# A two-block layer kernel: side work of the norm, the recurrent branch, the gates and the query and key sums put at other places of the order

## The reference

```
# first block
yg = (y.reshape(b, s, SSM_INNER) * jax.nn.silu(u_z))
yg = yg.reshape(b, s, SSM_GROUPS, SSM_INNER // SSM_GROUPS)
yg = yg * lax.rsqrt(jnp.mean(yg * yg, axis=-1, keepdims=True) + RMS_EPS)
y_a = yg.reshape(b, s, SSM_INNER) * norm_w             # gated norm
y_b = h * gelu(u_ly)                                   # recurrent branch
g = sigmoid(u_g.reshape(b, s, N_BRANCHES, D_MODEL) + gate_b)
merged = g[:, :, 0, :] * (y_a @ w_proj_ssm) + g[:, :, 1, :] * (y_b @ w_proj_lru)
# second block
q, k = _l2norm(silu(q)), _l2norm(silu(k))              # query and key sums
proj = einsum("btnc,ncd->btnd", stack([y_a, y_b, y_c, y_m]), w_up)
merged = sum(sigmoid(gate_logits.reshape(B, T, N_BRANCH, D)) * proj, axis=2)
```

## Time and profile before

| | |
|---|---|
| median of three runs | 921.43 us |
| the profiled execution | 918.49 us |
| its span, first to last instruction | 916.7 us |
| mean granted TensorE clock | 0.988 |
| TensorE busy (matmuls) | 880.7 us, 96% |
| VectorE busy | 636.8 us, 69% |
| ScalarE busy | 503.9 us, 55% |
| GpSimd busy | 77.0 us, 8% |
| DMA | 148.96 MB, mean 162 GB/s |

### The profile page before, as it was taken

How to read it: one execution, slowest core, us unless ns; L and a number is a source line. 1 busy time by engine, 2 the same in 40 slices (tenths; PEclk the granted TensorE clock), 3 DMA queues, 4 the chain that set the end, 5 groups by cost and what they waited for, 6 DMA issues and landing times.

```text
span 916.7 us, 15149 instructions
## 1 busy us (share of the span) xinstructions
PE 880.7 (96%) x6082; PEld 808.8 (88%) x6082; DVE 636.8 (69%) x1122; ACT 503.9 (55%) x792; POOL 77.0 (8%) x81
## 2 busy tenths in 40 slices
PE   6979999989999999999998998999999999999997
PEld 6979999989989999999996988999999777778885
DVE  6797987977878766566568895747555545666665
ACT  5555777645367656566568764424535424354543
POOL 0200002021020211111112003000000000000000
PEclk9999999989999999999999999999999999999999
DMA  9438433547454755555553546333333332346551
GB/s 346 148 135 292 154 139 115 183 144 271 140 185 163 246 170 187 199 176 189 192 182 127 182 162 227 127 108 115 98 110 99 105 120 83 124 143 217 191 162 46
DMA packets 40446, 148.96 MB, mean 162 GB/s; under 512 B 4506, under 2 KB 4664, under 8 KB 39736
## 3 DMA queue, kind: packets, MB, share of 16 engines
q1 hardware_dynamic: 40376, 147.99, 47.8%
HBM read 146.90 MB, written 1.08 MB: 161 GB/s over the span
## 4 chain that ended last, share of the span: by engine, by line
PE 80%; DVE 12%; ACT 5%; issue 2%; DMA 1%; SPq 0%; DVEq 0%; ACTq 0%
PE bank L603 36%; PE bank L598 14%; PE bank L599 14%; PE bank L600 14%; DVE t_wl L1700 4%; DVE t_arena L1715 3%; PE bank L606 2%; DVE t_arena L1705 1%; ACT t_arena L1228 1%; ACT t_wh L1223 1%; ACT t_hh L1228 1%; DVE t_sm L1712 1%; DVE t_x L1715 1%; DMA t_x<-in_xin 1%; DVE t_arena L1986 0%
## 5 line engine op out<-in xcount | busy, mean ns | idle before, releaser
L1700 DVE TENSOR_TENSOR t_wl<-t_raw,t_wh 128x1024 fp32r<-128x1024 f32 x260 | 316.7, 1226 | 128.2 <-ACT t_wh L1223 127.6
L598 PE MATMUL bank<-t_hh,t_wh 128*128 128x256 f32 x1240 | 360.9, 291 | 7.8 <-DVE t_wl L1700 4.1
L600 PE MATMUL bank<-t_hh,t_wl 128*128 128x256 f32 x1240 | 352.4, 284 | 0.0
L599 PE MATMUL bank<-t_hl,t_wh 128*128 128x256 f32 x1240 | 352.3, 284 | 0.0
L1223 ACT ACTIVATE t_wh<-t_raw 128x1024 fp32r<-128x1024 f32 x260 | 272.6, 1058 | 130.5 <-PE bank L600 72.1
L598 PEld LDWEIGHTS bank<-t_hh,t_wh 128*128 128x128 f32 x1240 | 239.3, 193 | 12.2 <-issue 6.1
L599 PEld LDWEIGHTS bank<-t_hl,t_wh 128*128 128x128 f32 x1240 | 239.4, 193 | 0.8
L600 PEld LDWEIGHTS bank<-t_hh,t_wl 128*128 128x128 f32 x1240 | 239.1, 193 | 0.0
L603 PE MATMUL bank<-t_wh,t_br 128*128 128x512 f32 x384 | 124.1, 393 | 2.2 <-ACT t_arena L1228 2.0
L1715 DVE SCALAR_TENSOR_TENSOR t_arena<-bank,t_par,t_arena 128x255 f32<-128x255 f32 (+1 forms) x180 | 73.4, 472 | 40.5 <-ACT t_arena L1228 40.5
L603 PEld LDWEIGHTS bank<-t_wh,t_br 128*128 128x128 f32 x384 | 72.1, 188 | 19.5 <-ACT t_arena L1228 2.9
(11 more groups left out here) (138 smaller groups left out, 858.4 us busy)
## 6 DMA issues: line engine op xcount, KB each, us to landing
t_raw<-in_ws SPq DMA_DIRECT2D x260, 512.0 KB, 4.0
t_br<-decay SPq DMA_DIRECT2D x1, 2048.0 KB, 10.4
t_arena<-in_post SPq DMA_DIRECT2D x3, 512.0 KB, 4.8
t_arena<-gates SPq DMA_DIRECT2D x1, 1536.0 KB, 10.5
t_x<-in_xin SPq DMA_DIRECT2D x4, 256.0 KB, 5.9
t_bd<-in_bd SPq DMA_DIRECT2D x1, 1024.0 KB, 11.3
t_x<-in_xtok SPq DMA_DIRECT2D x1, 1024.0 KB, 6.4
t_arena<-in_mem SPq DMA_DIRECT2D x1, 1024.0 KB, 9.7
```

The costliest lines, as they stand in the source:

```text
L598: e.matmul(o, wh, xh, start=first, stop=False, skip_group_check=True)
L599: e.matmul(o, wh, xl, start=False, stop=False, skip_group_check=True)
L600: return e.matmul(o, wl, xh, start=False, stop=last, skip_group_check=True)
L1700: e.tensor_tensor(WL[q % NS][:, :], RAW[q % NR][:, :], WH[q % NS][:, :].bitcast(F), SUB).then_inc(*lo.now(q))
```

## The change

It moves side work between ticks and engines; the arithmetic and the unit stream are the same.

- Norm: the gate products stand one per tick (45 to 48), the squares one per tick (46 to 49), the group sums at 49 and 51. TensorE's column sums are at tick 53, behind pl0's first unit, the spread at 55, the multiplies at 56 and 57, and the high and low halves behind pl2. SP's three loads stand two fetches later and wait for the sums too.
- Recurrent branch: the four low halves are made by VectorE at ticks 47 to 50.
- Gates at the end: for the second chunk the tangents stand before the last tick's lanes.
- Query and key sums: all eight tiles at tick 163.

VectorE's order ahead of pl0, before: from the split difference of tick 45 to the root chain's first step (t_wl is a split difference; waits on s_ssd_dve are gate products, on s_lru_act the branch's products, on s_ssd_act group sums).

The diff:

```diff
--- before.py
+++ after.py
@@ -479,7 +479,7 @@
         g_dn = tally("dn_pool")
         p_lru, a_lru, d_lru, g_lru = tally("lru_pe"), tally("lru_act"), tally("lru_dve"), tally("lru_pool")
         a_ya, d_ya, g_ya = tally("ya_hi"), tally("ya_lo"), tally("ya_lo2")
-        a_yb, g_yb = tally("yb_hi"), tally("yb_lo")
+        a_yb, d_yb = tally("yb_hi"), tally("yb_lo")
         a_mg, d_mg = tally("merged_hi"), tally("merged_lo")
         d_mem, a_mh, g_mh = tally("mem_normed"), tally("mem_hi"), tally("mem_lo")
         a_ns, d_ns, p_ht = tally("row_square"), tally("row_added"), tally("h_turned")
@@ -549,9 +549,10 @@
             e.dma_start(MSK, masks).then_inc(s_msk, 16)
             e.dma_start(bdT[:, :, :], bd).then_inc(s_bd, 16)
             for q in range(NR, NU):
-                if q == LAST["g7"] + NS + NR:
+                if q == LAST["g7"] + NS + NR + 2:
                     e.wait_ge(*p_ssd.of("y", 7))
                     e.wait_ge(*d_ssd.of("gated", 3))
+                    e.wait_ge(*p_ssd.of("gsum"))
                     e.dma_start(XT, xtok).then_inc(s_xt, 16)
                     e.dma_start(MEMF, min_).then_inc(s_mem, 16)
                     e.dma_start(POSTW["mixpost"], post[0]).then_inc(s_post["mixpost"], 16)
@@ -772,12 +773,12 @@
                 for t in range(8):
                     yield from walk.until(T_HEAD + 2 * t + 4)
                     y_pair(t)
-                yield from walk.until(48)
+                yield from walk.until(53)
                 e.wait_ge(*d_ssd.of("gsum", 1))
                 for g in range(2):
                     m = column_sums(3, 2 * g, [SSQ[:, 4 * g + k, :] for k in range(2)], g == 0, g == 1)
                 m.then_inc(*p_ssd.now("gsum"))
-                yield from walk.until(49)
+                yield from walk.until(55)
                 e.wait_ge(*d_rs.of("ssd"))
                 e.wait_ge(*d_ssd.of("cb", 1))
                 for g in range(2):
@@ -832,8 +833,6 @@
                 ps = dn_bank("nq")
                 e.wait_ge(*a_dn.of("sq", 1))
                 for t in range(8):
-                    if t == 4:
-                        yield
                     m = column_sums(ps, 2 * t, [DSQ[:, t, :]], t == 0, t == 7)
                 m.then_inc(*p_dn.now("nq"))
                 for i in range(4):
@@ -1099,7 +1098,7 @@
             walk.tick()
 
 
-            e.wait_ge(*g_yb.of(3))
+            e.wait_ge(*d_yb.of(3))
             for i in range(4):
                 chunk(f"pl{i}", YBh, YBl)
             e.wait_ge(*d_ya.of(6))
@@ -1339,8 +1338,8 @@
                     yield from walk.until(T_HEAD + h)
                     e.wait_ge(*d_ssd.of("seg", h))
                     act(DEC[h % 8], DEC[h % 8], ACT.Exp).then_inc(*a_ssd.now("exp", h))
-                yield from walk.until(45)
                 for t in range(4):
+                    yield from walk.until(46 + t)
                     sl = slice(2 * t, 2 * t + 2)
                     e.wait_ge(*d_ssd.of("gated", t))
                     act(SSQ[:, sl, :], XBC[:, sl, :], ACT.Square).then_inc(*a_ssd.now("sq", t))
@@ -1548,12 +1547,12 @@
 
             for i in range(4):
                 walk.cols(f"pl{i}")
-                if i == 1:
+                if i == 2:
                     for k in range(8):
                         e.wait_ge(*d_ssd.of("ya", k))
                         act(Hh[:, k, :], XBC[:, k, :], ACT.Copy).then_inc(*a_ya.now(k))
             e.wait_ge(s_mem, 16)
-            e.wait_ge(*g_yb.of(3))
+            e.wait_ge(*d_yb.of(3))
             for i in range(4):
                 act(MEMQ[:, 2 * i:2 * i + 2, :], MEMF[:, 2 * i:2 * i + 2, :], ACT.Square).then_inc(*a_sq.now("mem", i))
             for i in range(4):
@@ -1667,7 +1666,11 @@
                         if hf == 0 and i == SPLIT_AT[n]:
                             split_branch(at, n)
                         name = f"gt{n}_{hf}_{i}"
-                        walk.cols(name)
+                        if i == 0:
+                            walk.cols(name)
+                    walk.unit()
+                    walk.tick()
+                    walk.unit()
                     for tt in range(2):
                         e.wait_ge(*tokens_done(name, tt))
                         if at > 0:
@@ -1943,21 +1947,21 @@
                 skip(6)
                 yield from walk.until(44)
                 skip(7)
-                yield from walk.until(45)
                 for t in range(4):
+                    yield from walk.until(45 + t)
                     sl = slice(2 * t, 2 * t + 2)
                     e.wait_ge(*d_ssd.of("y", 2 * t + 1))
                     e.wait_ge(*d_ev.of(f"z{t}"))
                     stt(XBC[:, sl, :], XBC[:, sl, :], 0.5, ZS[:, sl, :], MUL, MUL).then_inc(*d_ssd.now("gated", t))
-                yield from walk.until(47)
                 for g in range(2):
+                    yield from walk.until(49 + 2 * g)
                     e.wait_ge(*a_ssd.of("sq", 2 * g + 1))
                     tt(SSQ[:, 4 * g:4 * g + 2, :], SSQ[:, 4 * g:4 * g + 2, :], SSQ[:, 4 * g + 2:4 * g + 4, :],
                        ADD).then_inc(*d_ssd.now("gsum", g))
-                yield from walk.until(48)
+                yield from walk.until(53)
                 rsqrt("ssd", NW, 3, 4, 512, p_ssd.of("gsum"))
                 for k in range(8):
-                    yield from walk.until(50 + k // 2)
+                    yield from walk.until(56 + k // 4)
                     if k == 0:
                         e.wait_ge(*p_ssd.of("grow"))
                     g = k // 4
@@ -1991,6 +1995,11 @@
                     e.wait_ge(*d_lru.of("h", q))
                     e.wait_ge(*a_lru.of("gelu", q))
                     tt(y, y, LY[:, 2 * q:2 * q + 2, :], MUL).then_inc(*d_lru.now("y", q))
+                for q in range(4):
+                    yield from walk.until(47 + q)
+                    sl = slice(2 * q, 2 * q + 2)
+                    e.wait_ge(*a_yb.of(q))
+                    tt(YBl[:, sl, :], XC[:, sl, :], YBh[:, sl, :].bitcast(F), SUB).then_inc(*d_yb.now(q))
                 yield
 
             def rows_lane():
@@ -2401,11 +2410,6 @@
                     sl = slice(2 * q, 2 * q + 2)
                     e.wait_ge(*a_lru.of("root"))
                     tt(ti[:, sl, :], ti[:, sl, :], XC[:, sl, :], MUL).then_inc(*g_lru.now("bx", q))
-                for q in range(4):
-                    yield from walk.until(45 + q)
-                    sl = slice(2 * q, 2 * q + 2)
-                    e.wait_ge(*a_yb.of(q))
-                    tt(YBl[:, sl, :], XC[:, sl, :], YBh[:, sl, :].bitcast(F), SUB).then_inc(*g_yb.now(q))
                 yield
 
             def rows_lane():
```

## The result

The changed kernel took **908.47 us** (median of four runs, 907.85 to 910.34), the kernel before beside it 920.93 (four runs, 919.01 to 922.85): a ratio of 0.9868, 95% interval 0.9842 to 0.9894, faster by 1.3%. The forecast was 911.3 in a range of 908.5 to 917.0, so the result is the range's low end itself, once rounded, and lies under the 909 to 913 that were given for the case in which all three parts come out as worked out. The profiled executions are closer to the working: 918.49 before, 907.85 after, 10.6 us less, where 10.1 were worked out.

The account below looks back on a forecast made before the run. TensorE, busy 880.7 of 916.7 us, was taken as the bound, so only its waits and low-clock time could be won: 7.0 - 0.4 + 1.5 + 2.0 = 10.1 us off the 921.43 median gave 911.3, range 908.5 to 917.

Parts of the forecast that it names:

- all three parts come out as worked out: The main forecast, gains at norm, query and key sums and last gates: 911.3 us, range 909 to 913, chance 0.51.
- A: Gated norm's column sums moved behind pl0's first unit: 4.01 us wait, 2.31 and 0.67 lost to the clock, 7.0 gained.
- less 0.4: Charge for pl0 waiting on the recurrent branch's last low half; ends 0 and 2.7 us.
- comes out about even with 2.95: VectorE's load before pl0: 3.3 us in the fullest unit, 2.6 in its neighbours, against a 2.95 us TensorE unit.
- Rival 2: VectorE pays for the low halves: pl0 waits 2.7 us instead of 0.4, time 913.6; chance 0.14.
- The slack before ps0, 2.9: Norm's low halves Hl end at 216.7, ps0 begins at 219.6: 2.9 us slack, no charge, but thin.
- rivals 3 and 4: 3: stall only moves to pl0, 917.9, chance 0.11. 4: VectorE's lateness paid twice, before pl0 and ps0, slower, chance 0.04.
- B: Query and key sums in one burst: row spread 1.5 us earlier, 1.0 of the 2.54 us wait remains, gain 1.5.
- a sign of being wrong: A wait over 2 us at pl0's or ps0's first matmul, or clock 0.50 behind the long burst.
- rival 1: The long burst of query and key sums lowers the clock: loses 1.1 us instead of gaining 1.5, 913.9; chance 0.2.
- C: Last projection's gates: tangents before their tick's side work remove two TensorE waits of 1.00 us, gain 2.0.
- the lower end: For the last projection's gates: gain 0, if ScalarE, waiting for the unit's end, starts something else late.

Follow-up runs that it names:

- e5: Changed kernel with the norm's column sums back before the first recurrent unit, products, squares and low halves kept as changed: 915.64 us, ratio 0.9953.
- e4: Changed kernel with the four gate products and their squares in one piece at tick 45 again: 910.36 us, ratio 0.9895.
- e3: Changed kernel with the recurrent branch's four low halves back on GpSimd, at ticks 45 to 48: 910.35 us, ratio 0.9880.
- e8: Changed kernel with the query and key sums one tick earlier (162), in one group of 32 records: 908.16 us, ratio 0.9874.
- e7: Changed kernel with the query and key sums one tick earlier (162) and in two halves again: 906.58 us, ratio 0.9867.
- e2: Changed kernel with the gates' tangents behind the side work of both ticks, as before the change: 910.76 us, ratio 0.9898.
- c1: The same kernel as e7, run again: 907.33 us, ratio 0.9858.
- c0: The changed kernel run once more, unaltered: 908.26 us, ratio 0.9886.
- e9: Changed kernel keeping only the norm sums' and spread's new place; products and squares in one piece, low halves on GpSimd, group sums at tick 47: 909.78 us.
- e1: Changed kernel with the query and key sums in two halves again: 910.42 us, ratio 0.9894.

## Why the prediction was right

**Where TensorE stands, not how much it does.** The reading from the earlier trace rows held: the matmuls are the same and the waits are gone.

**A, "4.01 + 2.31 + 0.67 = 7.0 us go", less 0.4.** That is 6.6; measured 6.76, once the start's 0.55 is taken off. e5 loses 7.5 with the sums put back and the companions kept. The clock term is right too: no window between 187 and 205 is below 1.00, and e4 shows the clock's price when a wait of 2.2 comes back. The new wait was put at 0.4 and is 0.32, in the row that was named; e3, without it, is 0.6 shorter, so it costs more than its bracket says.

**VectorE's load, "comes out about even with 2.95".** The fullest unit takes 2.94 us, not the 3.3 of the working. Rival 2 (VectorE pays for the low halves) wanted a wait of 2.7 before pl0; it is 0.32. VectorE's load is even lighter for the move, since GpSimd beside it had cost 1.1 us an operation. The prediction had set this against the rival only in passing. Still the rival was right about the sign: the low halves in VectorE's order are what TensorE waits for, and with GpSimd place A is 0.6 us shorter (e3). The move was not needed.

**The slack before ps0, 2.9.** It is 2.5: VectorE's last group of Hl ends at 215.86 (212.26 + 3.60), ps0 starts at 218.40. Nothing waited there, nor for SP's loads. With that, rivals 3 and 4 have no ground: the wait did not move, and nothing was late twice.

**B, "Gain 1.5", is the step that failed, in two ways.** The time: 0.9 was gained. The sums did come earlier by half a unit, 1.42 us, but "VectorE is idle and follows at once, so the row spread comes 1.5 us earlier" took the root chain's length for fixed. It was 3.98 us before and 4.50 after, and lies between 3.30 and 4.66 in the fourteen traces; that takes 0.52. The clock: the rest of the wait was to be 1.0 with the clock at 1.00; it is 0.31 with the clock at 0.50, which the prediction itself had named as a sign of being wrong. That is rival 1's mechanism, without its price: the rival charged the slow unit with 2.3 us, of which a wait of 1.0 hides part, and here the wait for the longer chain hides all of it. That this misreading of the clock cost nothing is luck; with no wait beside it the burst costs 1.47 us (e8 against e7), the whole gain. The choice against rival 1 went by 2.54 us of idle behind two groups of 16 that had not lowered the clock. That row is about idle time, and e8 shows that no idle is needed., put aside, were the nearer ones: same kind of records, no idle, clock 0.50. The Trainium skill, "TensorE: Matmul & The Clock Gate", section "Why this matters for your kernels", names idle gaps between bursts of matmuls as what lowers the clock in mid-kernel. The runs show a fall without one (e8), and the measurement decides.

**C, "1.00 us twice".** It is 1.29 twice (e2). The wait as the trace names it starts at the end of an overlapping matmul and leaves 0.3 out; the lower end did not come.

**The total.** 6.8 + 0.9 + 2.6 = 10.2 us by places, where 10.1 were forecast. So close a sum is partly luck: 0.6 too much in B and 0.6 too little in C cancel. That the medians differ by 12.5 is in how an execution stands to its median: the profiled one before lay 2.4 us under it, the one after 0.6 under. The size of the profiled gain was right; carrying it over to the median cost 1.8 us, and with it nearly the range. Why the two kernels' profiled executions lie so differently is not shown: of the kernel before only one was traced.

## What to carry to other kernels

Where the busiest engine waits for a short reduction in the middle of a dense stream, look for a product that does not need it and put the sums behind that: the place of the sums brought 5.9 us of 6.8 here. Do not gather one-column matmuls into one group to save a wait of a microsecond; issuing them a tick earlier, in two groups, takes the wait (all of it in e7, all but 0.34 in c1) and keeps the clock. GpSimd slows VectorE (1.1 us an operation here), and a lighter VectorE still helps only if what TensorE waits for comes sooner: the low halves on VectorE came later. The kernel with the sums early and split and the low halves on GpSimd was not run; e3 and e7 make it the next to try. And price a wait by the starts of the matmuls around it, not by its bracket: 1.00 in the bracket was 1.28.

## What was not expected of the hardware

- The granted clock fell to the 1.2 GHz level with TensorE busy in every window (e8), behind 32 one-column records in 3.63 us: eight traces of eight (in one, e3, within them), for 3 to 4 us, in e3 for twice that. With no wait to hide it this costs 1.47 us (e8 against e7). Behind two groups of 16, with a unit's half between, it never fell at that place.
- The thirteen small VectorE instructions of the root chain (16 columns each) took 3.30 us (e8) to 4.66 (c1) from execution to execution, 3.98 before and 4.50 after. No run shows why.
- In the delta-rule stretch (590 to 800 us), where groups of small matmuls abound, falls of the same kind come and go between executions of the same code. c0 has three, at 736, 750 and 774, where after has two; c1 has three at 736, 750 and 760, e7 two at 757 and 770:

```profile
758.00:760.00 2.00, 2.00 (x6) 0.50 0.12 12
...
770.00:772.00 2.00, 2.00 (x7) 0.63 0.01 4
```

  At about 1.5 us each they are a large part of the 2 to 6 us by which runs of one kernel differ. Stretches between two landmarks repeat to 0.1 us where no fall and no wait for the root chain lies in them, and are the better measure for a part worth 1 us.
- A wait of 1.14 us before pl0 (e9) left the clock at 1.00, one of 2.23 (e4) did not; the one of 2.54 at the row spread (before, e1) left it too. The length of a wait alone does not say it.
